# Delta rule: first two-row blocks by masked copies over identity blocks from ScalarE, and three steps one unit later

## What is computed

```python
decay = jnp.exp(jnp.where(incl, gc[..., :, None] - gc[..., None, :], -jnp.inf))
kb = k * beta
low = jnp.where(strict, jnp.einsum("bhnid,bhnjd->bhnij", kb, k) * decay, 0.0)
rhs = jnp.concatenate([v * beta, kb * jnp.exp(gc)[..., None]], axis=-1)
sol = lax.linalg.triangular_solve(low + jnp.eye(c, dtype=jnp.float32), rhs,
                                  left_side=True, lower=True, unit_diagonal=True)
```

## Time and profile before

| | us |
|---|---|
| median of 3 runs | 928.32 (927.93 to 928.45) |
| the profiled execution | 926.99 |
| its span | 925.2 |
| TensorE busy | 903.4 (98%) |
| VectorE busy | 472.1 (51%) |
| ScalarE busy | 505.6 (55%) |
| GpSimd busy | 674.7 (73%) |

### The profile page before, as it was taken

One profiled execution on the slowest core, in us unless ns is written; L12 is line 12 of the kernel. 1 busy time (PEld: TensorE's weight loads), 2 busy tenths in 40 slices (PEclk: granted clock), 3 DMA queues, 4 the chain that ended last, 5 costly groups with the idle time before them and its releaser, 6 DMA issues.

```text
span 925.2 us, 19503 instructions
## 1 busy us (share of the span) xinstructions
PE 903.4 (98%) x7764; PEld 836.4 (90%) x7764; DVE 472.1 (51%) x971; ACT 505.6 (55%) x712; POOL 674.7 (73%) x484
## 2 busy tenths in 40 slices
PE   6999899999999999999999999999999999999997
PEld 6999899998998889999999999888997899998886
DVE  4468745478343342777687776725656442220004
ACT  5674443663246456556776667556566365555331
POOL 5985556466655897967766787669797579889982
PEclk9999999999999999999999999999999999999999
DMA  8663333334333665644444544455563246656631
GB/s 314 218 217 126 120 127 121 113 122 153 117 115 114 214 200 164 207 157 141 143 132 159 162 138 152 146 193 187 170 204 101 91 144 223 195 190 204 203 118 45
DMA packets 41114, 147.16 MB, mean 159 GB/s; under 512 B 4544, under 2 KB 4672, under 8 KB 41024
## 3 DMA queue, kind: packets, MB, share of 16 engines
q1 hardware_dynamic: 39584, 141.76, 47.2%
q10 hardware_dynamic: 1440, 4.16, 1.3%
HBM read 144.86 MB, written 1.05 MB: 158 GB/s over the span
## 4 chain that ended last, share of the span: by engine, by line
PE 89%; DVE 5%; issue 2%; POOL 2%; ACT 2%; DMA 0%; DVEq 0%; ACTq 0%; POOLq 0%
PE dense L504 25%; PE dense L505 24%; PE dense L506 24%; PE bank L852 2%; PE bank L751 1%; POOL wlo L479 1%; PE bank L747 1%; PE bank L766 1%; PE dense L560 1%; POOL wlo L478 1%; DVE cv L1686 1%; PE bank L884 1%; PE bank L838 1%; PE bank L997 1%; PE bank L504 0%
## 5 line engine op out<-in xcount | busy, mean ns | idle before, releaser
L479 POOL TENSOR_TENSOR wlo<-raw,whi 128x512 fp32r<-128x512 f32 (+1 forms) x261 | 411.8, 1584 | 25.6 <-ACT whi L1112 25.5
L1112 ACT ACTIVATE whi<-raw 128x1024 fp32r<-128x1024 f32 (+1 forms) x264 | 275.2, 1056 | 236.1 <-PE dense L506 204.7
L478 POOL TENSOR_TENSOR wlo<-raw,whi 128x512 fp32r<-128x512 f32 x197 | 256.3, 1301 | 194.8 <-ACT whi L1112 194.7
L504 PE MATMUL dense<-x_hi,whi 128*128 128x256 f32 x1232 | 352.1, 286 | 8.1 <-DVE wlo L1617 7.1
L505 PE MATMUL dense<-x_lo,whi 128*128 128x256 f32 x1232 | 343.8, 279 | 0.0
L506 PE MATMUL dense<-x_hi,wlo 128*128 128x256 f32 x1232 | 343.7, 279 | 0.0
L504 PEld LDWEIGHTS dense<-x_hi,whi 128*128 128x128 f32 x1232 | 232.3, 189 | 12.5 <-DVE x_lo L1606 7.0
L505 PEld LDWEIGHTS dense<-x_lo,whi 128*128 128x128 f32 x1232 | 233.4, 189 | 0.7 <-issue 0.2
L506 PEld LDWEIGHTS dense<-x_hi,wlo 128*128 128x128 f32 x1232 | 232.7, 189 | 0.0
L504 PE MATMUL dense<-whi,ya_hi 128*128 128x512 f32 x192 | 77.4, 403 | 1.0 <-issue 0.8
L506 PE MATMUL dense<-whi,ya_lo 128*128 128x512 f32 x192 | 75.0, 391 | 0.0
(11 more groups left out here) (332 smaller groups left out, 1424.0 us busy)
## 6 DMA issues: line engine op xcount, KB each, us to landing
raw<-weight_units_dram SPq DMA_DIRECT2D x263, 512.0 KB, 3.7
xtok<-in_x_dram SPq DMA_DIRECT2D x1, 1024.0 KB, 6.8
gb<-in_ln_g_dram ACTq DMA_DIRECT2D x2, 512.0 KB, 4.6
gb<-in_ln_b_dram ACTq DMA_DIRECT2D x2, 512.0 KB, 7.2
out_dram<-zt SPq DMA_DIRECT2D x3, 256.0 KB, 2.0
qT<-x_turned_dram SPq DMA_DIRECT2D x2, 256.0 KB, 4.5
raw<-weight_units_dram SPq DMA_DIRECT2D x2, 256.0 KB, 4.9
qT<-x_turned_dram SPq DMA_DIRECT2D x1, 512.0 KB, 7.1
```

The source lines that it names most:

```text
L478: pool.tensor_tensor(wlo[:, slot, 0:half], unit_slot(u)[:, 0:half], whi[:, slot, 0:half].bitcast(F32), ALU.subtract)
L479: pool.tensor_tensor(wlo[:, slot, first:2 * half], unit_slot(u)[:, first:2 * half], whi[:, slot, first:2 * half].bitcast(F32), ALU.subtrac ...
L504: pe.matmul(out_, lh, rh, start=start, stop=False, skip_group_check=True)
L1112: act.activation(whi[:, u % NSPL, first:], unit_slot(u)[:, first:], ACT.Copy).then_inc(hi_done, 1)
```

## The change

Step 2 now reads, on VectorE: copy A to LT as before; wait for the identity blocks; copy the entries of A under a mask into the upper half of XN (two instructions, 64 rows each); signal TensorE; copy the entries of EL under a mask into the lower half of XN (two instructions); memset as before. ScalarE writes the identity blocks into both halves and both tiles of XN in one instruction (blank), a unit ahead of each half of the heads. The masks hold 1 where they held -1, and the sign is taken once, in step 1. The transposed blocks live in XN's upper half, where they lived in EL's. In the first half step 20 stands at unit 42, where it stood at 41; in the second half steps 1 and 2 stand at 46 and 47, where they stood at 45 and 46.

```diff
@@ -124,8 +124,8 @@
 
 GSTEPS = 21
 GDN_FIRST = (17, 44)
-GDN_BEHIND = [0, 1, 2, 4, 6] + list(range(7, 19)) + [19, 20, 22, 24]
-GDN_AT = {GDN_FIRST[half] + n: (half, s) for half in range(2) for s, n in enumerate(GDN_BEHIND)}
+GDN_BEHIND = [first + list(range(7, 20)) + [20, 22, last] for first, last in (([0, 1, 2, 4, 6], 25), ([0, 2, 3, 4, 6], 24))]
+GDN_AT = {GDN_FIRST[half] + n: (half, s) for half in range(2) for s, n in enumerate(GDN_BEHIND[half])}
 Q_SPREAD = 128.0
 PE_STEPS = [(s, g) for s in range(GSTEPS) for g in range(2) if (s, g) not in ((17, 1), (18, 0))]
 DVE_STEPS = PE_STEPS
@@ -200,8 +200,9 @@
         upto = con[:, C_UPTO:C_UPTO + P]
         after = con[:, C_AFTER:C_AFTER + P]
         ones = con[:, C_ONES:C_ONES + P]
-        neg = {s: con[:, C_NEG + i * 64:C_NEG + (i + 1) * 64] for i, s in enumerate(LEVELS[:6])}
-        neg1t = con[:, C_NEG1T:C_NEG1T + 64]
+        low = {s: con[:, C_NEG + i * 64:C_NEG + (i + 1) * 64] for i, s in enumerate(LEVELS[:6])}
+        low1 = low[1].bitcast(I32)
+        low1t = con[:, C_NEG1T:C_NEG1T + 64].bitcast(I32)
         ident64 = con[:, C_BLOCK:C_BLOCK + 64]
         pick = {s: con[:, C_PICK + 192 * i:C_PICK + 192 * (i + 1)].bitcast(I32) for i, s in enumerate((1, 4, 16))}
         dist = con[:, C_DIST:C_DIST + 3 * P]
@@ -321,6 +322,7 @@
         ya_done = sem("ya_done")
         ya_hi_done = sem("ya_hi_done")
         ya_ready = sem("ya_ready")
+        unit_blocks = sem("unit_blocks")
         gdn_gates = sem("gdn_gates")
         gdn_products = sem("gdn_products")
         gdn_vector = sem("gdn_vector")
@@ -741,14 +743,14 @@
                         elif s == 14:
                             last = pe.matmul(block(A, u, 1), block(LT[:, g, :], u, 0, 256), block(XN[:, g, :], u, 0), start=True, stop=True)
                         elif s == 15:
-                            last = pe.matmul(block(B, u, 0), block(EL[:, g, :], u, 1), block(EL[:, g, :], u, 1, 256), start=True, stop=True)
+                            last = pe.matmul(block(B, u, 0), block(EL[:, g, :], u, 1), block(XN[:, g, :], u, 1, 256), start=True, stop=True)
                         elif s < 16 and s % 2 == 0:
                             for b in range(2):
                                 last = pe.matmul(block(A, u, b), block(LT[:, g, :], u, b), block(XN[:, g, :], u, b), start=True, stop=True)
                         elif s < 15:
                             lv = LEVELS[(s - 5) // 2 + 1]
                             for b in range(2):
-                                last = pe.matmul(B[64 * b:64 * b + 64, u * 32:(u + 1) * 32], block(EL[:, g, :], u, b, 256),
+                                last = pe.matmul(B[64 * b:64 * b + 64, u * 32:(u + 1) * 32], block(XN[:, g, :], u, b, 256),
                                                  even_odd(block(EL[:, g, :], u, b), lv, 0), start=True, stop=True)
                         elif s == 16 and g == 0:
                             last = pe.matmul(A[:, o], unit(XT[:, 0, :], u), unit(VB[:, 0, :], u), start=True, stop=True)
@@ -1259,6 +1261,14 @@
                 settle(h_copied)
                 act.activation(bank[1][:, T:2 * T], bank[1][:, T:2 * T], ACT.Silu).then_inc(h_copied, 1)
                 settle(h_copied)
+
+            def blank(half):
+                act.wait_ge(consts_loaded, 16)
+                if half:
+                    act.wait_ge(gdn_products, pe_step(0, 19, 1))
+                act.activation(XN[:, :, :].rearrange("p g (u c) -> p g u c", c=64),
+                               ident64.unsqueeze(1).unsqueeze(1).broadcast_to([P, 2, 8, 64]), ACT.Copy).then_inc(unit_blocks, 1)
+                settle(unit_blocks)
 
             def ya_first(j):
                 act.wait_ge(ya_u, j + 1)
@@ -1319,6 +1329,7 @@
                         act.activation(gt[:, 6, :, :], SB[3][:, 0:2 * GH].rearrange("p (t h) -> p t h", t=2), ACT.Exp).then_inc(gate_exp, 1)
                         settle(gate_exp)
                     key_norms(GDN_FIRST.index(n + 1))
+                    blank(GDN_FIRST.index(n + 1))
                     if n + 1 == GDN_FIRST[1]:
                         act.wait_ge(lb_diff, 1)
                         act.activation(lbc[:, 0:2, :], lbc[:, 0:2, :], ACT.Exp).then_inc(lb_exp, 1)
@@ -1725,7 +1736,7 @@
                         vec.tensor_tensor(four(AT[:, g, :]), four(B[:, :]), all4(upto), ALU.mult).then_inc(gdn_vector, 1)
                         settle(gdn_vector)
                     elif s == 1:
-                        link(vec.tensor_tensor(EL[:, g, :], A[:, :], EL[:, g, :], ALU.mult))
+                        link(vec.scalar_tensor_tensor(EL[:, g, :], A[:, :], -1.0, EL[:, g, :], ALU.mult, ALU.mult))
                         vec.tensor_tensor(AT[:, g, :], B[:, :], AT[:, g, :], ALU.mult).then_inc(gdn_vector, 1)
                         settle(gdn_vector)
                     elif s == 2:
@@ -1735,13 +1746,13 @@
                         upper, lower = slice(0, 64), slice(64, P)
                         link(vec.tensor_copy(LT[upper, g, :].rearrange("p (h u c) -> p h u c", h=2, u=4),
                                              A[upper, :].rearrange("p (u h c) -> p h u c", u=4, h=2)))
-                        vec.tensor_copy(blocks(LT[lower, g, :]), four(A[lower, :])[:, :, 64:P]).then_inc(gdn_vector, 1)
+                        link(vec.tensor_copy(blocks(LT[lower, g, :]), four(A[lower, :])[:, :, 64:P]))
+                        vec.wait_ge(unit_blocks, half + 1)
+                        link(vec.copy_predicated(blocks(XN[upper, g, :], 256), all64(low1t, upper), four(A[upper, :])[:, :, 0:64]))
+                        vec.copy_predicated(blocks(XN[lower, g, :], 256), all64(low1t, lower), four(A[lower, :])[:, :, 64:P]).then_inc(gdn_vector, 1)
                         settle(gdn_vector)
-                        link(vec.tensor_tensor(blocks(XN[upper, g, :]), four(EL[upper, g, :])[:, :, 0:64], all64(neg[1], upper), ALU.mult))
-                        link(vec.tensor_tensor(blocks(XN[lower, g, :]), four(EL[lower, g, :])[:, :, 64:P], all64(neg[1], lower), ALU.mult))
-                        link(vec.tensor_tensor(blocks(XN[:, g, :]), blocks(XN[:, g, :]), all64(ident64), ALU.add))
-                        link(vec.tensor_tensor(blocks(EL[:, g, :], 256), blocks(LT[:, g, :]), all64(neg1t), ALU.mult))
-                        link(vec.tensor_tensor(blocks(EL[:, g, :], 256), blocks(EL[:, g, :], 256), all64(ident64), ALU.add))
+                        link(vec.copy_predicated(blocks(XN[upper, g, :]), all64(low1, upper), four(EL[upper, g, :])[:, :, 0:64]))
+                        link(vec.copy_predicated(blocks(XN[lower, g, :]), all64(low1, lower), four(EL[lower, g, :])[:, :, 64:P]))
                         link(vec.memset(four(XT[lower, g, :])[:, :, 0:64], 0.0))
                     elif s == 3:
                         link(vec.tensor_tensor(four(KX[:, g, :]), four(A[:, :]), heads(g, 6 + g, half), ALU.mult))
@@ -1753,19 +1764,19 @@
                     elif s < 16:
                         lv = LEVELS[(s - 4) // 2 + 1]
                         if s == 4:
-                            vec.tensor_tensor(blocks(EL[:, g, :]), blocks(A), all64(neg[lv]), ALU.mult).then_inc(gdn_vector, 1)
+                            vec.tensor_tensor(blocks(EL[:, g, :]), blocks(A), all64(low[lv]), ALU.mult).then_inc(gdn_vector, 1)
                             settle(gdn_vector)
                         elif s % 2 == 0:
                             if s == 14:
-                                link(vec.tensor_scalar(EL[64:P, g, 0:256], A[64:P, 0:256], -1.0, None, ALU.mult))
+                                link(vec.tensor_copy(EL[64:P, g, 0:256], A[64:P, 0:256]))
                             else:
-                                link(vec.tensor_tensor(blocks(EL[:, g, :]), blocks(A), all64(neg[lv]), ALU.mult))
+                                link(vec.tensor_tensor(blocks(EL[:, g, :]), blocks(A), all64(low[lv]), ALU.mult))
                             vec.wait_ge(gdn_products, pe_step(half, s, g))
-                            vec.tensor_copy(columns(EL[:, g, 256:512], lv // 2, 1), columns(B[:, 0:256], lv // 2, 1)).then_inc(gdn_vector, 1)
+                            vec.tensor_copy(columns(XN[:, g, 256:512], lv // 2, 1), columns(B[:, 0:256], lv // 2, 1)).then_inc(gdn_vector, 1)
                             settle(gdn_vector)
                             if s == 14:
-                                link(vec.tensor_copy(four(XT[0:64, g, :])[:, :, 0:64], blocks(EL[0:64, g, :], 256)))
-                                link(vec.tensor_copy(four(XT[64:P, g, :])[:, :, 64:P], blocks(EL[64:P, g, :], 256)))
+                                link(vec.tensor_copy(four(XT[0:64, g, :])[:, :, 0:64], blocks(XN[0:64, g, :], 256)))
+                                link(vec.tensor_copy(four(XT[64:P, g, :])[:, :, 64:P], blocks(XN[64:P, g, :], 256)))
                         else:
                             o = columns(XN[:, g, 0:256], lv, 0)
```

(4 more changed lines are left out.)

## The result

| | before | after |
|---|---|---|
| median, us | 928.38 (927.93 to 929.66, 4 runs) | 923.74 (923.34 to 924.63, 4 runs) |
| ratio | | 0.9943, 95% interval 0.9931 to 0.9956 |
| the profiled execution, us | 926.99 | 923.9 |
| its span, us | 925.2 | 922.1 |
| VectorE busy, us | 472.1 | 461.3 |

The changed kernel is faster by 0.57%.

A forecast was written before the change was run, and what follows sets the result against it. TensorE was taken as the bound, idle 6.3 us between 60 and 230 us. Gains of 2.9 and 0.55 us make 3.45, carried from the profiled execution to the median of 928.32: 924.9 us, range 922.2 to 927.6.

The forecast's parts named there:

- VectorE's work in the first half: Behind step 2, masked copies replace longer operations; TensorE's waits of 1.87, 0.77 and 0.26 us go, gain 2.9 us.
- The second pair: The two predicated copies from EL behind the signal to TensorE: 2.8 us in the first half's second tile, beside GpSimd.
- The identity blocks: ScalarE's copy into XN: 1.06 us, nothing before the first half, full cost on the way to AT before the second.
- Step 20: First half, unit 41 to 42: freed pair's wait goes, gain 1.0 us; next half's exponentials 2.5 late, at 192.0.
- Steps 1 and 2: Second half, one unit later: new TensorE waits of 1.1, 0.4 and 1.25 us at steps 1 to 3; half gains 0.55.
- B: Second half loses 1.35 us as its first tile's EL copies meet GpSimd; total -1.55, 926.8 us; chance 0.2.
- D: Slower: every predicated copy queues behind GpSimd, step 3 of the second half waits 6.9 us; 931.9 us; chance 0.08.
- C: The added second-half waits don't arise and all 6.3 us go: 922.0 us; chance 0.2.
- E: Nothing that shows, since a wait downstream takes the gain back: 928.3 us; chance 0.05.
- The sum: Both halves together: 2.9 + 0.55 = 3.45 us off the profiled execution of 926.99 us.
- I carry the difference to the median: The 3.45 us off the profiled execution was taken off the median of 928.32 us too, giving 924.9.
- The cap: TensorE's 6.3 us of idle time between 60 and 230 us was called the limit on any gain.

The follow-up runs named there:

- e12: The kernel before with only the unused SiLU table load behind step 20 of the first half left out; 926.92 us, ratio 0.9979.
- e10: The changed kernel with all steps at the old units, second half's identity blocks written at unit 40, unused SiLU table load left out; 919.83 us, ratio 0.9896.
- e1: The kernel before with the three steps moved to their new units and nothing else changed; 928.30 us, ratio 0.9992.
- e7: The changed kernel with the second half's identity blocks written at unit 41 and its step 3 at unit 49 instead of 48; 926.13 us, ratio 0.9965.
- e9: The same kernel as e7, with the unused SiLU table load behind step 20 of the first half left out; 924.21 us, ratio 0.9946.
- e0: The changed kernel run again as it is, against the kernel before on the same chip; 923.67 us, ratio 0.9939.

## Why the prediction was right, step by step

**VectorE's work in the first half.** Right: waits of 1.87, 0.77 and 0.26 us are gone. The price of the copies from the bank (0.45) and the order of the events hold. The second pair was set at 2.8 us and took 1.24, because GpSimd happened to idle 0.74 us there; so VB had about 1.5 us to spare, not 0.3. That margin was luck. Beside GpSimd in the second half such a pair took 2.5, as set. What the Trainium skill (SBUF — State Buffer, Who interferes with whom) says of one and of two SBUF inputs holds for predicated copies here: 0.45 against 1.09 and 1.41.

**The identity blocks.** Right: 1.06 us, hidden in the first half, in full on the way to AT in the second. The doubled copy (1.44 to 2.5) shows it, the early one (to 0.4) as well. That ScalarE "does not idle at all" there was not quite so: it pauses 0.25 us for VectorE's VB, ahead of the blocks, so the price stays.

**Step 20.** Right in both directions: the freed pair's wait goes, the exponentials come later. The trace of after is 3.48 us ahead at that place, so 188.59 is 192.07 in the frame of before, against 192.0 on record.

**Steps 1 and 2.** Right: new waits of 1.44, 0.26 and 1.19, forecast as 1.1, 0.4 and 1.25. Rivals B and D, which needed slow copies ahead of the signal, fall with the rows above; C with the waits that did arise; E with the measured gain.

**The sum.** 3.45 us of TensorE's idle time, 2.99 in the trace (3.4 without the wait of 0.4 at step 0). In the trace this is right to half a microsecond. The profiled executions themselves are 3.1 us apart.

**The step that was mis-sized** is the last: "I carry the difference to the median". 3.45 of 928.38 is a ratio of 0.9963, outside the measured interval. It rested on the sentence that the granted clock is 1.00 in all these stretches, "so none of the price is a clock's", which holds for the one execution that was traced and not for the others. A price that it left out is the fall of the clock behind the waits for VB: 1.2 us for the one fall in the moves-alone trace, 1.07 and 1.63 for the two in e12's. The only trace of before has none, so how often before pays it is read from mean clocks alone. It isn't the whole of the missing microsecond as far as these runs go, since executions of before at 0.998 lie anywhere from 926.76 to 929.61 us; what else sets them apart stays open.

**The cap** was too low as well: "These 6.3 us are the cap on any gain here." e10 removes 6.1 of them; its profiled execution is 7.5 us shorter than that of before, and its ratio of 0.9896 is 9.7 us of that chip's 929.99.

## What to carry to other kernels

A move in a schedule by hand should be costed against the engine whose chain ends last there (here ScalarE's 14 us between two steps, with an unused table load in it); a move that needs a second one to make up its cost is a sign that the chain, not the place of the steps, is what to shorten. A wait can be worth more than its length, above all where the clock falls behind it, so compare the clock of all executions, not only of the traced one, and don't take the idle time for the cap. Put work for which an engine is not needed at once into a stretch where it waits anyway.

## What the runs showed of the hardware

**TensorE's granted clock.** Behind waits of 1.87 and 0.77 us at step 4 it fell to 0.50 for 3 to 4 us in one execution (e1) and stayed at 1.00 in another with the same code in that stretch (before). In e12 it fell behind 1.88 and 0.77 and again behind 0.98 and 0.77; behind 2.0 and 0.8 at step 4 of the second half it was at 0.50 for 6 to 7 us in one execution (e7) and for some 3 in another (e9). The first of these falls cost 1.2 us, the two of e12 1.07 and 1.63.

**TensorE's pace at a full clock.** In the changed kernel's trace a group of three dense matmuls (L506 to L508; the first of each is shown) takes 0.34 us from start to start at 96.16 and 0.35 at 208.58, both at a granted clock of 1.00:

```profile
96.16 0.28 PE L506 MATMUL dense<-x_hi,whi 128*128 128x256 f32 x1
96.50 0.28 PE L506 MATMUL dense<-x_hi,whi 128*128 128x256 f32 x1
...
208.58 0.28 PE L506 MATMUL dense<-x_hi,whi 128*128 128x256 f32 x1
208.93 0.28 PE L506 MATMUL dense<-x_hi,whi 128*128 128x256 f32 x1
```

Before runs at the quicker pace from 217 to 260 us; after runs there mostly at the slower one. TensorE is 3.80 us ahead of before at step 5 of the second half, and 3.12 at step 16, with no wait in between, so 0.7 us of the gain was given back in pace. That isn't a price of waiting less: in the second trace of the same kernel (e0), with the same waits, the pace is the quicker one there and the lead stays at 3.52 us from step 5 to step 14, and in e10's, which waits least, at 7.57. What sets the pace stays open.
